# Two modulation blocks of a one-core layer stack moved from TensorE in the FFN to VectorE beside the output tiles

## The chip, the cores and the metric

One core of one Trainium2 chip runs one program. The metric is the device time of one launch in microseconds; less is better.

## The reference, cut to what matters

The input has 256 tokens of width 2048. A first block (pooling, convolution and gated branches, then an FFN of inner width 5504) is followed by two layers of a second block, which also carry a 256-token context beside the tokens. Everything is float32. The part that the change touches is the modulation of the second block:

```python
for l in range(DEPTH_2):
    shift, scale, gate = jnp.split(sc @ w_ada[l] + b_ada[l], 3, axis=-1)
    shift_c, scale_c, gate_c = jnp.split(scc @ w_ada[l] + b_ada[l], 3, axis=-1)
    h = rms(x, norm_w[l]) * (1.0 + scale[:, None]) + shift[:, None]
    hc = rms(xc, norm_w[l]) * (1.0 + scale_c) + shift_c
    ...
    x = x + gate[:, None] * merge_out(o_a, o_b, o_c, z, w_out[l])
    if not last:
        ...
        xc = xc + gate_c * merge_out(oa_c, ob_c, oc_c, z_c, w_out[l])
```

`sc` and `scc` are vectors of length 2048 (SiLU of `c` and `c_ctx`), so each product with `w_ada[l]` (2048 x 6144) is a matrix times a vector: 50 MB of weights a layer, read once, for two result vectors. Layer 1 is the last, so its context is not updated and its gate is needed for the tokens alone, while its shift is needed for tokens and context.

## The kernel before, in words

**The stream of weights.** All weights stand in one DRAM array in the order of use, cut into quarters of 128 x 1024 float32 (512 KB). SyncE loads quarter n into slot n mod 8 of `raw` as soon as quarter n-8 has been used (`weights_used`, L830; the few loads outside its loops are L844). For an ordinary quarter ScalarE writes the rounded high part `whi` (L865, four slots, three quarters ahead) and VectorE the remainder `wlo` (L1330, written over `raw`); TensorE then multiplies high by high, high by low and low by high. "hi" and "lo" below are these two conversions. A tile is 128 output channels and mostly takes two quarters.

**The modulation** has 24 blocks of 512 columns, of 8 quarters each. They are worked off in two ways:

- In the five FFN groups (`MOD_GROUPS`, `weave`, `mod_quarters` at L2215) a quarter needs no conversion: TensorE multiplies it by the columns `cs`, two quarters at a time, between two tiles. After 8 quarters VectorE copies the rows (L1745), TensorE transposes them (`mod_fold`, L2224), and VectorE sums them into `ada_t` (L1754, L1758). An FFN group has 16 up tiles, then 16 down tiles of one quarter each. A list says how many modulation quarters follow each tile; the last group has 32 of them, the other four 24 each: 128 quarters, that is 16 blocks.
- As rows on VectorE: a quarter holds half of the input for 128 output columns, and one `tensor_tensor_reduce` ("a product" below, with the reading of its accumulator) multiplies it by the broadcast vector and sums it, started from the bias or from the first half's sum. This is `gate0_products` beside the tiles of c0 (L1843), `gate1_products` beside those of c1 (L1857) and `row_products` beside layer 0's output tiles (L2112). A shift row of layer 1 needs two products a quarter (tokens and context), a gate row of layer 1 one.

TensorE holds back the last matmul of a tile that has such rows until the products are made (`gate0_mods`, `gate1_mods`, `gate_mods`), since that matmul also releases the rows' slots.

**Layer 0's output tiles** (out0: 16 tiles, each 48 matmuls of 512 columns) have `MOD_OUT` quarters of rows: none at tile 0, then 2, 2, 3 repeated to tile 13, 2 at tile 14, none at tile 15. `OUT_ROWS` alternates one shift row (two products a quarter) with one gate row (one product), 48 products in all. Per tile t, VectorE does in this order: the products of tile t, lo of quarters 2t+2 and 2t+3, the scaling of X by `fin_rst` (L2082), and then, once TensorE has finished tile t, `out_tile` (L2097) and a drain. GpSimd adds one square per tile (L2760).

**Layer 1's output tiles** (out1: 16 tiles, each 16 matmuls of 512 and 16 of 256 columns, `wide_chunk`, L2186 and L2187) have no rows. VectorE does lo of 2t+3 and 2t+4, then `out_tile` (L2091, L2093). The first 6 of 16 chunks of tiles 0 and 1 are computed inside the attention of heads c; `out_chunks` finishes them, and `tiles` does the rest, in a loop of four tiles a turn from tile 4 on. The stream's first 8 quarters of out1 are in their slots before out1 begins.

c1 has 16 quarters of gate rows 8 to 15, beside its 11 tiles (`C1_WEAVE`).

## Time and profile before

| | us |
|---|---|
| median of 3 runs (lowest, highest) | 3282.17 (3281.78, 3285.78) |
| the profiled execution's own time | 3282.73 |
| its span, first to last instruction | 3280.9 |
| PE busy | 3241.9 |
| VectorE busy | 2276.1 |
| ScalarE busy | 1431.5 |
| bytes read from HBM | 550.33 MB |

The profiled execution is 0.56 us above the median, and 1.8 us of its time lie outside the span. TensorE's granted clock is 0.999 of full over the whole span. PE stands for TensorE's matmuls, DVE for VectorE, ACT for ScalarE, POOL for GpSimd and SP for SyncE; a "q" behind a name is the engine's sequencer. Start times count from the first instruction of the span. An idle time in square brackets lies before the row's instruction and names what ended it.

### The profile page before, as it was taken

How to read it: one execution, taken by the hardware profiler on the slowest of the kernel's cores; microseconds unless marked ns; L12 is line 12 of the kernel's file. 1: busy time of each engine (PE TensorE's matmuls, PEld its weight loads, DVE VectorE, ACT ScalarE, POOL GpSimd, SP SyncE). 2: the span in 40 equal slices, each digit the busy share in tenths (PEclk: the TensorE clock that was granted, in tenths of full speed). 3: DMA queues.
4: the chain of work that ended last, by engine and by line, in shares of the span. 5: the costliest groups of instructions: out<-in, count | busy, mean ns of one | idle time of the engine just before them, and what ended most of it. 6: DMA issues, size and time to landing. Idle time of an engine off the chain costs nothing.

```text
span 3280.9 us, 56206 instructions
## 1 busy us (share of the span) xinstructions
PE 3241.9 (99%) x20346; PEld 2780.6 (85%) x20346; DVE 2276.1 (69%) x3372; ACT 1431.5 (44%) x2193; POOL 611.7 (19%) x552
## 2 busy tenths in 40 slices
PE   8999999999999999999999999999999999999999
PEld 8999999998987787898888787778878888888878
DVE  7887877567776677776765566667568776775865
ACT  5444445545443343453543433532352453453353
POOL 4999930111440000000300000000001100000000
PEclk9999999999999999999999999999999999999999
DMA  6555555565577777777733222134325543333435
GB/s 219 183 182 181 186 186 183 185 211 185 198 250 253 253 251 263 242 249 271 262 103 100 75 90 76 54 124 149 109 85 206 204 149 116 129 97 122 165 106 172
DMA packets 159872, 559.78 MB, mean 171 GB/s; under 512 B 17552, under 2 KB 23840, under 8 KB 159264
## 3 DMA queue, kind: packets, MB, share of 16 engines
q1 hardware_dynamic: 154144, 534.67, 48.4%
q0 software_dynamic: 5504, 22.04, 2.0%
q8 instruction: 151, 2.47, 0.3%
q14 instruction: 73, 0.60, 0.1%
HBM read 550.33 MB, written 6.31 MB: 170 GB/s over the span
## 4 chain that ended last, share of the span: by engine, by line
PE 91%; DVE 4%; ACT 2%; DVEq 1%; issue 1%; DMA 1%; ACTq 1%; POOL 0%; SPq 0%
PE psum L2159 17%; PE psum L2163 17%; PE psum L2160 17%; PE psum L2186 15%; PE psum L2187 7%; PE psum L2370 4%; PE psum L2521 2%; PE psum L2547 2%; PE psum L2532 2%; PE psum L2215 2%; PE psum L2371 2%; DVE wlo L1330 1%; PE psum L2290 1%; DVEq L1316 1%; PE psum L2478 1%
## 5 line engine op out<-in xcount | busy, mean ns | idle before, releaser
L865 ACT ACTIVATE whi<-raw 128x1024 fp32r<-128x1024 f32 (+3 forms) x844 | 864.6, 1030 | 982.5 <-PE psum L2163 538.8
L1330 DVE TENSOR_TENSOR wlo<-raw,whi 128x1024 fp32r<-128x1024 f32 (+3 forms) x844 | 1027.9, 1225 | 372.2 <-ACT whi L865 342.0
L2159 PE MATMUL psum<-hcat,whi 128*128 128x256 f32 (+1 forms) x3436 | 1125.8, 328 | 7.2 <-DVE wlo L1330 3.5
L2163 PE MATMUL psum<-hcat,wlo 128*128 128x256 f32 (+1 forms) x3436 | 1109.7, 323 | 2.0 <-DVE gate_half L1857 1.5
L2160 PE MATMUL psum<-hcat,whi 128*128 128x256 f32 (+1 forms) x3436 | 1109.3, 323 | 0.0
L2186 PE MATMUL psum<-hcat,whi 128*128 128x512 f32 x2048 | 725.8, 398 | 0.1
L2159 PEld LDWEIGHTS psum<-hcat,whi 128*128 128x128 f32 x3436 | 653.2, 190 | 78.1 <-issue 25.6
L2163 PEld LDWEIGHTS psum<-hcat,wlo 128*128 128x128 f32 x3436 | 653.0, 190 | 53.8 <-issue 2.3
L2160 PEld LDWEIGHTS psum<-hcat,whi 128*128 128x128 f32 x3436 | 653.6, 190 | 49.3 <-issue 0.7
L2187 PE MATMUL psum<-hcat,wlo 128*128 128x256 f32 x2048 | 573.5, 280 | 0.0
L2186 PEld LDWEIGHTS psum<-hcat,whi 128*128 128x128 f32 x2048 | 384.5, 188 | 107.3 <-issue 17.2
L2187 PEld LDWEIGHTS psum<-hcat,wlo 128*128 128x128 f32 x2048 | 386.6, 189 | 0.1
L2721 POOL TENSOR_SCALAR tap<-glu,par 128x255 f32<-128x255 f32 (+9 forms) x150 | 203.8, 1358 | 0.3 <-issue 0.3
L2370 PE MATMUL psum<-thirdcat,whi 128*128 128x512 f32 x512 | 182.9, 401 | 0.0
L2708 POOL TENSOR_TENSOR thirdcat<-tmp,thirdcat 128x256 fp32r<-128x256 f32 x43 | 51.3, 1193 | 617.8 <-ACT thirdcat L919 617.8
L2723 POOL TENSOR_TENSOR conv<-conv,tap 128x255 f32<-128x255 f32 (+9 forms) x150 | 149.2, 994 | 22.1 <-issue 0.3
L2371 PE MATMUL psum<-thirdcat,wlo 128*128 128x256 f32 x512 | 142.9, 279 | 0.0
L2370 PEld LDWEIGHTS psum<-thirdcat,whi 128*128 128x128 f32 x512 | 96.1, 188 | 39.7 <-DVE X L1712 9.2
L1361 DVE RECIPROCAL rst<-rst 128x512 f32<-128x512 f32 (+1 forms) x39 | 106.8, 2738 | 27.5 <-ACT rst L894 27.5
L2760 POOL TENSOR_TENSOR racc<-racc,rsq 128x256 f32<-128x256 f32 (+1 forms) x64 | 79.9, 1248 | 244.3 <-ACT rsq L931 221.8
L1893 DVE COPY qkv<-psum 128x512 f32<-128x512 f32 (+1 forms) x78 | 49.5, 635 | 107.6 <-PE psum L2163 107.5
L1951 DVE TENSOR_REDUCE stat<-psum 128x2 f32<-128x1024 f32 x78 | 81.6, 1046 | 34.6 <-PE psum L2521 30.5
(305 smaller groups left out, 3610.7 us busy)
## 6 DMA issues: line engine op xcount, KB each, us to landing
raw<-in_stream SPq DMA_DIRECT2D x978, 512.0 KB, 4.1
raw<-in_stream SPq DMA_DIRECT2D x18, 384.0 KB, 3.0
raw<-in_stream SPq DMA_DIRECT2D x24, 256.0 KB, 2.9
resid_dram<-X POOLq DMA_DIRECT2D x2, 2048.0 KB, 9.4
crow<-c_dram POOLq DMA_DIRECT2D x4, 1024.0 KB, 9.3
bias<-in_natten POOLq DMA_DIRECT2D x16, 256.0 KB, 2.9
X<-resid_dram POOLq DMA_DIRECT2D x4, 1024.0 KB, 6.2
raw<-in_stream SPq DMA_DIRECT2D x16, 192.0 KB, 2.6
```

Source lines behind the costliest of these rows:

```text
L865: act.activation(whi[:, c % HI_SLOTS, 0:n], raw[:, slot, 0:n], ACT.Copy).then_inc(hi_ready, 1)
L1330: vec.tensor_tensor(wlo[:, slot, 0:n], raw[:, slot, 0:n], whi[:, c % HI_SLOTS, 0:n].bitcast(F32), ALU.subtract).then_inc(lo_ready, 1)
L1361: vec.reciprocal(r, r)
L2159: pe.matmul(dst, h, cat[:, kk, c0:c0 + width], start=(q == 0 and k == 0), stop=False)
L2160: pe.matmul(dst, h, cat[:, kk, c0 + loff:c0 + loff + width], start=False, stop=False)
L2163: last = pe.matmul(dst, l_, cat[:, kk, c0:c0 + width], start=False, stop=(q == nq - 1 and k == nch - 1))
L2186: pe.matmul(psum[:, bank, :].rearrange("p (l c) -> p l c", l=2), h, both, start=first, stop=False)
L2187: return pe.matmul(psum[:, bank, 0:S], l_, both[:, 0, :], start=False, stop=last)
L2370: pe.matmul(psum[:, bank, :], h, thirdcat[:, kk, :], start=first, stop=False)
L2371: return pe.matmul(psum[:, bank, 0:S], l_, thirdcat[:, kk, 0:S], start=False, stop=last)
L2721: pool.tensor_scalar(tap[:, t % 2, 0:S - t], pick(glu, c, 0, S - t), wt, None, ALU.mult)
L2723: pool.tensor_tensor(pick(conv, c, t, S), pick(conv, c, t, S), tap[:, t % 2, 0:S - t], ALU.add)
```

## The change

Layer 1's gate rows leave out0; all 16 of its shift rows are made there instead (64 products in place of 48, in the same 32 quarters). c1 now makes gate rows 0 to 7 and out1 makes gate rows 8 to 15: 16 new quarters in out1's stream (two behind tile 1, two behind tile 2, one behind each of tiles 3 to 14), with one product each. Two blocks (16 quarters) leave the last FFN group, which keeps 16. The stream's length stays the same. In out1 TensorE's and ScalarE's loops become straight code, and the last chunk of each tile that has rows waits for them.

```diff
-MOD_FFN = [0, 2, 2, 0, 2, 2, 2, 0, 2, 2, 0, 2, 2, 2, 0, 2] + [0] * LATE + [2, 0] * 5 + [0] * 3
 MOD_FEW = [0, 2] * 8 + [0] * LATE + [0, 2, 0, 0, 2, 0, 0, 2, 0, 2, 0, 0, 0]
-MOD_GROUPS = [MOD_FEW if g < FF_GROUPS - 1 else MOD_FFN for g in range(FF_GROUPS)]
+MOD_LEAST = [0, 2, 0, 0, 2, 0, 0, 2, 0, 0, 2, 0, 0, 2, 0, 0] + [0] * LATE + [2, 0, 0, 2, 0, 0, 2] + [0] * 6
+MOD_GROUPS = [MOD_FEW if g < FF_GROUPS - 1 else MOD_LEAST for g in range(FF_GROUPS)]
...
-OUT_BLOCKS = [4 * D // 512 - 2, 4 * D // 512 - 1]
+OUT_BLOCKS = [*range(3 * D // 512, 4 * D // 512)]
...
-_shift, _gate = [4 * b + i for b in OUT_BLOCKS for i in range(4)], [5 * KD + t for t in range(KD // 2)]
-OUT_ROWS = [(j, 2 - n, half_) for some in zip(_shift, _gate) for n, j in enumerate(some) for half_ in range(2)]
-C1_ROWS = [5 * KD + t for t in range(KD // 2, KD)]
+OUT_ROWS = [(4 * b + i, half_) for b in OUT_BLOCKS for i in range(4) for half_ in range(2)]
+LAST_ROWS = [5 * KD + t for t in range(KD)]
 C1_WEAVE = weave([2] * 11, [1, 1, 2, 1, 2, 1, 2, 1, 2, 1, 2])
+OUT1_WEAVE = weave([2] * KD, [0, 2, 2] + [1] * (KD - 4) + [0])
...
                 if l:
-                    plain(f"out{l}", 32, 8, peel=1)
+                    plain("out1", 32, 32)
...
-                        s, (j, n, half_) = Q0["out0"] + pos, OUT_ROWS[a]
+                        s, (j, half_) = Q0["out0"] + pos, OUT_ROWS[a]
                         vec.wait_ge(raw_in[s % SLOTS], 16 * (s // SLOTS + 1))
-                        for c in range(n):
+                        for c in range(2):
...
-                def out_tiles(i):
-                    for k in range(8):
-                        lo(C0["out1"] + k + AHEAD, 8 * i)
-                        if k % 2 == 1:
-                            out_tile(1, 4 * i + k // 2, BANK[T0["out1"] + k // 2], Q0["out1"] + k, 8 * i)
-                            vec.drain().then_inc(x_tile, 1)
-
                 if l:
-                    out_tiles(0)
...
+                    for t, e in enumerate(OUT1_WEAVE):
+                        gate1_products("out1", e, KD, row_product.rearrange("p (b c) d -> p b c d", c=1)[:, t % 2])
+                        lo(C0["out1"] + 2 * t + AHEAD)
+                        lo(C0["out1"] + 2 * t + 1 + AHEAD)
+                        out_tile(1, t, BANK[T0["out1"] + t], Q0["out1"] + e["pos"] + 1, 0)
+                        vec.drain().then_inc(x_tile, 1)
...
                     if rows and kk == KD - 1:
-                        pe.wait_ge(gate_mods, rows[-1][1] + 1)
+                        pe.wait_ge(gate1_mods if l else gate_mods, (KD if l else 0) + rows[-1][1] + 1)
...
                         if kk % 8 == 7:
-                            last.then_inc(weights_used, 1)
+                            last.then_inc(weights_used, 1 + (len(rows) if kk == KD - 1 else 0))
...
                 if l:
-                    for t in range(2):
-                        out_chunks(l, t, Y_EARLY, KD)
-                    tiles("out1", 16, 4, hcat, 0, 2 * S, w, skip=2, k0=Y_PLACE, wide=True)
+                    for t, e in enumerate(OUT1_WEAVE):
+                        out_chunks(l, t, Y_EARLY if t < 2 else 0, KD, rows=e["mods"])
                     continue
```

The rest of the diff renames `gate1_products`'s arguments (it takes the phase's name, the first row and the scratch it writes to), sets the phases' lengths, and puts the quarters into the stream in the new order.

## Rows read from the trace of the kernel before

**Rows 1.** The page, part 1: busy us (share) xinstructions of each engine.

```profile
PE 3241.9 (99%) x20346; PEld 2780.6 (85%) x20346; DVE 2276.1 (69%) x3372; ACT 1431.5 (44%) x2193; POOL 611.7 (19%) x552
```

**Rows 2.** Three stretches: span, each engine's busy us (instructions), clock, DMA share, GB/s.

```profile
2458.00:2599.00 141.00, 141.00 (x625) 116.68 (x624) 115.14 (x155) 36.68 (x53) 23.80 (x14) 1.00 0.60 209
3199.50:3272.00 72.50, 72.50 (x412) 62.86 (x412) 43.31 (x53) 25.52 (x25) 0.00 (x0) 1.00 0.56 184
1472.00:1622.00 150.00, 150.00 (x1107) 128.34 (x1106) 106.28 (x175) 68.08 (x95) 34.01 (x23) 1.00 0.79 273
```

**Rows 3.** Waits of PE over the whole span: us in total, times, longest us.

```profile
PE psum L2163 <- DVE gate_half L1857: 1.5, 1, 1.5
...
PE psum L2634 <- DVE ada_t L2112: 1.0, 1, 1.0
```

**Rows 4.** The same view of the last FFN group, modulation matmuls of L2215 alone.

```profile
1472.00:1622.00 150.00, 17.04 (x128) 2.52 (x128) 1.00 0.79 273
```

**Rows 5.** Chain that ended last, last FFN group: start us, us, what.

```profile
1502.91 0.99 PE psum L2215 x8
1509.86 0.99 PE psum L2215 x8
1522.56 0.99 PE psum L2215 x8
1529.50 0.44 PE psum L2224 x4
```

**Rows 6.** PE in order of time at the end of that group: start us, us.

```profile
1621.78 0.60 PE L2224 MATMUL psum<-con,arow 128*128 128x128 f32 x4
1622.14 0.36 PE L2267 MATMUL psum<-hcat,whi 128*128 128x256 f32 x1
```

**Rows 7.** PE in order of time, 3.3 us later.

```profile
1625.48 0.67 PE L2290 MATMUL psum<-racc,con 128*128 128x256 f32 x2 [0.23 <-POOLq L2816]
```

**Rows 8.** VectorE in order of time, one output tile (the eighth) of layer 0.

```profile
2522.45 0.88 DVE L2097 SCALAR_TENSOR_TENSOR X<-psum,ada_t,X 128x256 f32<-128x256 f32 x2 [1.71 <-PE psum L2163]
2523.57 1.29 DVE L2112 CUSTOM_DVE_ANT_0 row_product<-raw,crow,par 128x1024 f32<-128x1024 f32 x1 [0.24 <-issue]
...
2524.99 2.10 DVE L2112 CUSTOM_DVE_ANT_0 row_product<-raw,crow_ctx,par 128x1024 f32<-128x1024 f32 x1
...
2529.85 0.08 DVE L2112 DVE_READ_ACCUMULATOR2_ANT ada_t<- 128x1 f32 x1
...
2532.12 0.48 DVE L2082 SCALAR_TENSOR_TENSOR X<-X,par,fin_rst 128x256 f32<-128x256 f32 x1
2533.34 0.88 DVE L2097 SCALAR_TENSOR_TENSOR X<-psum,ada_t,X 128x256 f32<-128x256 f32 x2 [0.73 <-PE psum L2163]
```

**Rows 9.** Waits of all engines during layer 0's output tiles (2445 to 2620 us).

```profile
DVE X L2097 <- PE psum L2163: 17.0, 11, 3.6
...
DVE wlo L1330 <- ACT whi L865: 1.3, 4, 0.4
```

**Rows 10.** VectorE in order of time during layer 1's output tiles.

```profile
3197.27 2.36 DVE L1330 TENSOR_TENSOR wlo<-raw,whi 128x1024 fp32r<-128x1024 f32 x2
...
3204.12 0.48 DVE L2091 SCALAR_TENSOR_TENSOR X<-psum,ada_t,X 128x256 f32<-128x256 f32 x1 [0.51 <-PE psum L2187]
...
3205.30 1.23 DVE L1330 TENSOR_TENSOR wlo<-raw,whi 128x1024 fp32r<-128x1024 f32 x1
...
3209.77 0.48 DVE L2091 SCALAR_TENSOR_TENSOR X<-psum,ada_t,X 128x256 f32<-128x256 f32 x1 [0.51 <-PE psum L2187]
```

**Rows 11.** ScalarE in order of time at the same place.

```profile
3194.93 2.01 ACT L865 ACTIVATE whi<-raw 128x1024 fp32r<-128x1024 f32 x2 [0.54 <-PE psum L2187]
...
3206.94 1.06 ACT L865 ACTIVATE whi<-raw 128x1024 fp32r<-128x1024 f32 x1 [1.76 <-PE psum L2187]
```

**Rows 12.** DMA issues of layer 1's output tiles: xcount, KB each, median us to landing.

```profile
raw<-in_stream SPq DMA_DIRECT2D x20, 512.0 KB, 4.3
```

**Rows 13.** The same of the last FFN group.

```profile
raw<-in_stream SPq DMA_DIRECT2D x77, 512.0 KB, 5.3
```

More of the change, by code:

```diff
@@ L157 @@
     PHASES += [(f"z{_l}", 2 * _n[0] + Z_MODS[_l], _n[0]), (f"a{_l}", 24, 12), (f"za{_l}", 2 * _n[1] + row_mods(f"za{_l}"), _n[1]),
-               (f"b{_l}", 20, 10), (f"zb{_l}", 2 * _n[2] + row_mods(f"zb{_l}"), _n[2]), (f"c{_l}", 22 + (2 * len(C1_ROWS) if _l else row_mods("c0")), 11), (f"kvb{_l}", 12, 12),
-               (f"qb{_l}", 9, 9), (f"out{_l}", 32 + (0 if _l else sum(MOD_OUT)), 16)]
+               (f"b{_l}", 20, 10), (f"zb{_l}", 2 * _n[2] + row_mods(f"zb{_l}"), _n[2]), (f"c{_l}", 22 + (KD if _l else row_mods("c0")), 11), (f"kvb{_l}", 12, 12),
+               (f"qb{_l}", 9, 9), (f"out{_l}", 32 + (KD if _l else sum(MOD_OUT)), 16)]
 Q0, T0 = {}, {}
@@ L202, in _converted @@
             own = {pos for e in Z_WEAVE[l] for pos, _ in e["pre"] + e["mods"]}
-        elif name in ROW_WEAVE or name in ("c1", "out0"):
-            own = {pos for e in ROW_WEAVE.get(name, C1_WEAVE if name == "c1" else OUT_WEAVE) for pos, _ in e["mods"]}
+        elif name in ROW_WEAVE or name in ("c1", "out0", "out1"):
+            own = {pos for e in dict(ROW_WEAVE, c1=C1_WEAVE, out0=OUT_WEAVE, out1=OUT1_WEAVE)[name] for pos, _ in e["mods"]}
         of += [Q0[name] + k for k in range(nq) if k not in own]
@@ L1845, in gate0_products, with gate1_products @@
                     last.then_inc(gate0_mods, 1)
-            def gate1_products(e):
+            def gate1_products(name, e, first, out):
                 for pos, a in e["mods"]:
-                    s, (t, half_) = Q0["c1"] + pos, divmod(a, 2)
-                    j = C1_ROWS[t]
+                    s, (t, half_) = Q0[name] + pos, divmod(first + a, 2)
+                    j = LAST_ROWS[t]
                     vec.wait_ge(crow1_in, 16)
@@ L2622, in out_chunks @@
                         pe.wait_ge(lo_ready, s + kk // 8 + 1)
-                    if kk in [first for first, _ in YCAT]:
+                    if t < 2 and kk in [first for first, _ in YCAT]:
                         pe.wait_ge(ycat_lo, len(YCAT) * l + sum(first <= kk for first, _ in YCAT))
                     if rows and kk == KD - 1:
-                        pe.wait_ge(gate_mods, rows[-1][1] + 1)
+                        pe.wait_ge(gate1_mods if l else gate_mods, (KD if l else 0) + rows[-1][1] + 1)
                     h, l_ = weight(s + kk // 8, P * (kk % 8))
@@ L2904, in _stream @@
     rows_c = rows[ROW_OF].transpose(2, 0, 1, 3).reshape(-1, P, QW)
-    rows_out = np.concatenate([rows[j, :, half_][None] for j, _, half_ in OUT_ROWS])
-    rows_c1 = rows[C1_ROWS].transpose(0, 2, 1, 3).reshape(-1, P, QW)
+    rows_out = np.concatenate([rows[j, :, half_][None] for j, half_ in OUT_ROWS])
+    rows_last = rows[LAST_ROWS].transpose(0, 2, 1, 3).reshape(-1, P, QW)
     def put_woven(weave_, tiles_, mods):
@@ L2950, in _stream @@
         if l:
-            put(oq)
+            put_woven(OUT1_WEAVE, oq, rows_last[KD:])
         else:
```

9 lines of the change are left out of this document (3 added, 6 removed).

## The prediction

> **What bounds the kernel now.** I read the page first. TensorE is busy for 3241.9 of 3280.9 us [rows 1], so what leaves TensorE shortens the kernel, as long as nothing else has to wait for the engine that takes it. VectorE takes it, so the second question is how much room VectorE has at the three places of the change. The view of three stretches [rows 2] says that TensorE is busy without a gap in layer 0's output tiles, in layer 1's and in the last FFN group, while VectorE is at 115.1 of 141 us, 43.3 of 72.5 and 106.3 of 150. An average doesn't tell whether another product fits, because VectorE works in order and waits for TensorE at the end of every tile. So I read on in the waits of the first stretch and in VectorE's order of time, tile by tile; their rows come with the terms below. TensorE already waits for products at two places, 1.5 us in c1 and 1.0 us at out0's tile 1 [rows 3].
>
> **What leaves the FFN.** The last group has 128 modulation matmul records, 8 for each pair of quarters, so 16 pairs [rows 4]; 8 pairs go. The price of one comes from the spacing of three pairs: 6.95 us across one tile and a pair, 12.70 us across two tiles and a pair [rows 5]. So a tile takes 5.75 and a pair 1.20 us, and eight take 9.6 us. Two of four folds go too, at 0.44 us where they stand in the chain [rows 5]. I credit only one: the last of the four stands behind the last tile [rows 6], and 3.3 us later TensorE waits 0.23 us for GpSimd's sum [rows 7], which comes from the tile before and not from the fold, so that wait grows by most of what the fold gives up. Sum: -10.0 us (-9.6 without any fold, -10.5 with both). TensorE never waits in this group [rows 2], so no wait is there to take the matmuls' place, and VectorE and the queue of SyncE's loads get less to do there (two copies and sums, 16 loads). The pair behind the last up tile goes too, which covered the last piece that GpSimd makes for the down tiles; the first seven chunks of three down tiles still cover it (21 chunks, each the 16th part of a tile's 5.75 us, 7.5 us in all), and if they didn't, it would cost no more than that pair's 1.2 us.
>
> **What out0 gets.** 16 more products, all at tiles 2 to 14 (tile 1 keeps its four). Between the starts of two products lie 1.42 us (2523.57 to 2524.99 [rows 8]), the reading of the accumulator among them; the second there is stretched to 2.10 us by GpSimd's sum of the tile, of which there is one a tile whatever the products. So 16 x 1.42 = 22.7 us of work are added to VectorE. Its slack from tile 2 to tile 14 is what it waited for TensorE, 17.0 us in 11 waits, and at most 1.3 us for ScalarE [rows 9]. So VectorE's work exceeds the room by 22.7 - 17.0 - 0.7 = 5.0 us, if no slack is wasted, taking half of the wait for ScalarE as usable.
>
> To see what TensorE feels of it I carried four rules through the tiles. TensorE's tile takes 10.89 us (2522.45 to 2533.34, the starts of two out_tiles [rows 8]). VectorE starts its products 1.12 us after the start of the last out_tile (2522.45 to 2523.57), has its first lo 1.14 us behind the last product, and comes to the next out_tile 2.83 us behind it (2.27 for two lo and 0.56 for the scaling). TensorE's tile t ends no sooner than 0.33 us after its products (one of 48 matmuls, 0.23, and 0.1 for the signal, my estimate), and tile t+1 starts no sooner than the lo of quarter 2t+2. For each tile I kept the duration measured there with its long instruction (thirteen tiles, of which [rows 8] show one) and added 1.42 us per new product. With the old counts the rules give tile 14's end at 2598.6 us, where the trace has 2598.62. With the new ones a tile with 2 quarters needs 10.2 to 10.5 us of VectorE, one with 3 needs 13.1 to 13.4, so three tiles need about 34 us against TensorE's 32.7. VectorE falls back by 1.1 to 1.4 us in every three tiles, and TensorE waits at two places in each: 0 to 0.8 us for the products before the last matmul of the 3-quarter tile, and 0.9 to 1.4 us for the first lo behind it. Tile 15 starts at 2603.8 instead of 2598.2: **+5.6 us**. With 1.36 or 1.50 us a product it is +5.0 or +6.6; with 0.2 us more or less a tile, +7.4 or +4.5.
>
> **What out1 gets.** Per tile TensorE takes 5.65 us (3204.12 to 3209.77 [rows 10]). VectorE's own work is 1.18 us from the start of an out_tile to the next lo (3204.12 to 3205.30), two lo of 1.14 each, and now one product of 1.42: 4.9 us, so it keeps up from tile 3 on, with 0.7 us to spare. Tiles 1 and 2 have two products. Tile 0 ends at 3194.9 (ScalarE is released by it [rows 11]), and tile 1, of which only 10 chunks are left, at 3198.4. But VectorE comes free from tile 0 at 3197.27 [rows 10], so two products end at 3200.2 and the last chunk at 3200.65: 2.3 us late. Tile 2 then has its products at 3206.95 (two lo, an out_tile and two products after 3200.2) where its matmuls would be ready for them at 3205.9: 1.1 us late; tile 3 is 0.2 us late, and the rest is on time. **+3.6 us.**
>
> This holds while the loads come in time. Three quarters a tile are 1.57 MB in 5.65 us, 278 GB/s, where now 184 are moved [rows 2]. A quarter takes a median of 4.3 us to land in out1 now [rows 12] and 5.3 us in the last FFN group [rows 13], which moves 273 GB/s. The first quarter of tile t+3 takes the slot of the second of tile t, so it is asked for at the end of tile t. It has then to land, to pass hi (1.06 [rows 11]) and lo (1.14), and behind it come the out_tile and the products for which tile t+2 waits, 10.86 us after the request. That leaves 10.86 - 1.06 - 1.14 - 1.18 - 1.52 - 0.1 = 5.9 us for landing. At 4.3 us I get +3.6, at 5.3 +5.2, at 5.9 +6.4. I take 4.3: the requests come two and one at a time, spread over the tile, as in out1 now, while the FFN group's come in larger bursts. The least is 2.3 us (tile 1 alone). The last tile has no rows, so the end behind it stays.
>
> On the landing the Trainium skill ("DMA: Bandwidth & Descriptors", Anatomy of one DMA) has its own figure: about 2.0 us fixed plus the bytes over 436 GB/s, so some 3.2 us for a quarter as an estimate. By it out1 would lose 3.1 us instead of 3.6 and the sum be 0.5 us lower. The rows here say 4.3, and I go by them.
>
> **Edits at nothing.** c1 keeps 16 quarters and 16 products, only of other rows. The straight code of out1 is hidden as out0's is, where TensorE runs straight code without a gap [rows 2]; a loop turn saved may give back 0.1 us. The gates that out1 makes are made in order ahead of the out_tile that reads them. Scratch for out1's products is in SBUF as at L2112.
>
> **Sum.** -10.0 + 5.6 + 3.6 = -0.8 us. On the profiled execution's 3282.73 us that is 3281.9; on the median, 0.56 us lower, **3281.4 us**. About 0.2%, or 6.6 us, is what a measurement of this kernel can tell from no change, so the forecast is "no difference": the FFN's gain is given back beside the output tiles. By the bounds (-10.5 to -9.6, +4.5 to +7.4, +2.3 to +6.4) this case reaches from 3278.5 to 3286.4.
>
> **Rivals.**
> - *VectorE has the room.* If the averages count (VectorE at 82% in out0, 60% in out1) and the order within a tile doesn't, nothing is given back: -10.0, 3272.2 us. For it: waits of VectorE for TensorE in 11 of 13 tiles [rows 9]. Against it: their sum is 17.0 us, less than the 22.7 added. Chance 0.13.
> - *Slower: the ring of slots in out1.* If quarters land 7 us after the request instead of 4.3, the loop over two tiles (request, landing, hi, lo, out_tile, product) is longer than two tiles. Each microsecond above 5.9 then costs half a microsecond a tile, over twelve tiles, and the late loads of the first tiles come on top: the same steps give +13.7 for out1, in all +9.3, 3291.5 us. It decides from 5.9 us on, and reaches a total above +6.6 at 6.6. For it: 5.3 us at 273 GB/s [rows 13]. Against it: the median there is still below the threshold, and DMA engines are at 79% of their time [rows 2]. Chance 0.10.
> - *The FFN doesn't give the time.* If the loads pace the last group (79% DMA share), the removed matmuls leave waits: at worst 0 instead of -10.0, so +9.2, 3291.4 us. Against it: no idle time of TensorE in the stretch, and the loads become 16 fewer. Chance 0.05.
> - The forecast's case has 0.72.
>
> **Numbers.** The range goes from 3275.5 to 3289.5: my case with its bounds, and the part of the rivals in which a stall is half missing or half as large again. Outside lie most of the first rival and the ends of the two others, about 0.2. Faster by over 0.2%: 0.14 (the first rival and a little of mine). Slower: 0.14 (the two others, less what stays within 6.6 us). Same: 0.72.
>
> **What would show it.** In the profile after: 64 matmul records of L2215 in the last FFN group, and out0's first tile about 10 us earlier. The products of out0 x64 with VectorE's waits for TensorE at L2097 down from 17.0 us to nearly nothing; TensorE idle at its tiles' last matmul and first matmul, 5 to 6 us in all, in pairs around tiles 3, 6, 9 and 12. In out1 two waits of TensorE of about 2.3 and 1.1 us at tiles 1 and 2 and none later, with quarters landing in 4 to 5 us. The forecast is wrong if out0's stretch grows by less than 3 or more than 8 us, if out1 shows waits at every second tile, or if the FFN group shrinks by less than 9 us.

## Result, and the profile after

The changed kernel takes 3286.73 us (median of 20 runs, 3283.54 to 3290.07) where the kernel before took 3281.98 beside it (20 runs, 3280.18 to 3285.78): +4.8 us, a ratio of 1.0015 [1.0009, 1.0020]. Run again on another chip it was +7.2 us, 1.0021 [1.0012, 1.0030]. The forecast was -0.8 us, no difference. The time lies inside the range and within 0.2%, but it grew, by more than its interval, where I had the gain and the loss cancel.

The profiled execution took 3283.54 us, the shortest of the 20, with a span of 3281.7 us. The page, part 1 (answers to [rows 1]), then the three stretches of [rows 2], moved to where they now lie (the first is the last FFN group, which I end at 1611 where it has ended; the second and third are layer 0's and layer 1's output tiles):

```profile
PE 3233.7 (99%) x20274; PEld 2778.3 (85%) x20274; DVE 2314.0 (71%) x3426; ACT 1430.1 (44%) x2193; POOL 612.1 (19%) x552
```

```profile
1472.00:1611.00 139.00, 139.00 (x1027) 125.14 (x1026) 104.84 (x167) 66.34 (x93) 33.63 (x23) 1.00 0.70 231
2449.00:2590.00 141.00, 138.05 (x602) 112.54 (x601) 129.89 (x179) 34.64 (x51) 23.09 (x14) 1.00 0.59 204
3199.50:3272.00 72.50, 69.82 (x403) 60.80 (x403) 60.16 (x80) 27.40 (x26) 0.00 (x0) 1.00 0.81 289
```

TensorE lost 8.2 us of busy time, and the span did not get shorter. In the FFN group it still never waits. In both output stages it now does: 141.00 busy of 141 has become 138.05, and 72.50 of 72.5 has become 69.82, while VectorE rose from 115.1 to 129.9 us and from 43.3 to 60.2. In out1 the DMA share went from 0.56 to 0.81.

The waits of PE over the whole span (answers to [rows 3]; us in total, times, longest), then VectorE's waits from the start of out0 on. The last row is before's, for the same load:

```profile
PE psum L2181 <- DVE ada_t L1857: 4.6, 2, 2.7
...
PE psum L2629 <- DVE ada_t L2112: 2.7, 1, 2.7
```

```profile
DVE X L2082 <- DMA X<-in_ctxT: 3.0, 1, 3.0
...
DVE X L2097 <- PE psum L2158: 1.7, 5, 0.7
```

```profile
DVE X L2082 <- DMA X<-in_ctxT: 1.4, 1, 1.4
```

VectorE's waits for TensorE at L2097 are down from 17.0 us [rows 9] to 1.7, as the working said: its slack is used up. But TensorE's wait at out0's tile 1 grew from 1.0 to 2.7 us, which no step of mine had. The cause stands in the other row: VectorE waits 3.0 us, where it was 1.4, for context rows that are loaded into X ahead of tile 0. The issues before and after:

```profile
X<-in_ctxT POOLq DMA_DIRECT2D x2, 1024.0 KB, 9.7
```

```profile
X<-in_ctxT POOLq DMA_DIRECT2D x2, 1024.0 KB, 11.3
```

The first is before's row, the second after's. The same load is issued at the same distance from its neighbours and lands 1.6 us later. In all eleven traces with the shortened FFN it took 11.0 to 11.8 us (median of the two loads), in all five with more quarters there (before's three, b4 and c3) 9.3 to 9.7. Why is open.

**Where the time went, by stage.** Five landmarks of VectorE, the same in each kernel, cut the span: its reciprocal behind the FFN, the update of X at out0's first tile and at its fifteenth, and at out1's first and last. Lengths in us, one profiled execution each:

| kernel | start to reciprocal | to out0 | out0 | to out1 | out1 |
|---|---|---|---|---|---|
| before | 1627.1 | 821.7 | 149.8 | 597.1 | 81.9 |
| before, again (b1) | 1627.3 | 821.6 | 149.8 | 599.1 | 80.3 |
| after | 1616.1 | 823.4 | 155.4 | 598.2 | 85.4 |
| after, again (a1) | 1616.3 | 822.9 | 156.4 | 598.2 | 86.6 |

Against the mean of the two traces of before (1627.2, 821.7, 149.8, 598.1, 81.1) the mean of the two of after has -11.0, +1.5, +6.1, +0.1 and +4.9: together +1.6 us. The two profiled executions of the changed kernel were the shortest of their 20 and 11, those of before were not, so this is the lower end of the difference.

The traces of the experiments below have most stages unchanged, and they show how far one stage scatters. Means over all traces in which a stage is as in the kernel of its row (number of traces in brackets; the changed kernel's out0 with all 64 products, its out1 with all 16, none filled):

| kernel | start to reciprocal | to out0 | out0 | to out1 | out1 |
|---|---|---|---|---|---|
| before | 1627.0 (3) | 821.6 (3) | 149.8 (2) | 598.4 (3) | 80.8 (3) |
| changed | 1617.2 (11) | 823.2 (11) | 155.8 (6) | 598.7 (11) | 86.8 (4) |
| difference | -9.8 | +1.6 | +6.0 | +0.3 | +6.0 |

Together +4.1 us, near the first pair of medians (+4.8) and inside the interval of each (+3.0 to +6.6 and +3.9 to +9.8). The two pairs above came out lower by chance: their first stage, 1616.1 and 1616.3 us, is at the short end of eleven (1616.1 to 1619.1, the same work in each), and before's out1 of 81.9 us is the long one of three. In that trace TensorE takes 5.65 us a tile there and in b1 5.55, both at a granted clock of 1.00; why is open.

**What fills the rest.** The granted clock is below 1.00 in short stretches, 1 us windows in the trace of after behind the wait at out0's tile 1 (columns: window, its length, PE busy (instructions), clock, DMA share, GB/s):

```profile
2444.00:2446.00 2.00, 0.00 (x0) 1.00 0.78 301
2446.00:2447.00 1.00, 0.86 (x2) 0.56 0.06 25
2447.00:2448.00 1.00, 1.00 (x3) 0.50 0.02 8
2448.00:2449.00 1.00, 1.00 (x4) 0.50 0.20 29
2449.00:2450.00 1.00, 1.00 (x5) 0.73 0.86 287
2450.00:2451.00 1.00, 1.00 (x6) 1.00 0.99 381
```

TensorE did nothing for 2.7 us, and then the granted clock was 0.50, the 1.2 GHz level, before it came back to 1.00 (2.4 GHz). The shortfalls of the four windows add up to 0.44 + 0.50 + 0.50 + 0.27 = 1.7 us of full clock. Such stretches, nearly all with 1.7 us lost (a3 has one of 3.4), start in or just behind TensorE's gaps of 1.8 to 3.3 us, at most places in some executions and not in others: before at 844 (gap 2.2 us), before again at 2672 (2.9) and 3065 (1.9) and not at 844, after at 2446 and 2668. At out0's tile 1 it stands in all nine traces whose gap there is 2.2 us or more, and in none of the others (gap 0.7 to 1.0 us, or filled, or gone). Over the timed executions the mean clock is 0.9992 for before (33 runs, beside a1) and 0.9980 for after (20), and the changed kernel's time goes with it: 3284.1 us on average at 0.999, 3287.1 at 0.998, 3289.4 at 0.997. So the change had added a place where the clock falls, and two more gaps in out1 of that size, and the question for the experiments was how much of the loss is that, and how much is VectorE, its order, and the loads.

### The profile page after: what moved, and what is told of

It is laid out like the page before. It is cut to its first block, busy times and chain, and to the rows that moved or that the text cites. A ratio compares the mean times of both kernels' runs of the same rounds, so it can differ in the third digit from the quotient of the medians.

```text
span 3281.7 us, 56108 instructions
## 1 busy us (share of the span) xinstructions
PE 3233.7 (99%) x20274; PEld 2778.3 (85%) x20274; DVE 2314.0 (71%) x3426; ACT 1430.1 (44%) x2193; POOL 612.1 (19%) x552
## 4 chain that ended last, share of the span: by engine, by line
PE 89%; DVE 5%; ACT 2%; DVEq 1%; issue 1%; DMA 1%; ACTq 0%; POOL 0%; SPq 0%
PE psum L2154 17%; PE psum L2158 17%; PE psum L2155 17%; PE psum L2181 14%; PE psum L2182 7%; PE psum L2365 4%; PE psum L2516 2%; PE psum L2542 2%; PE psum L2527 2%; PE psum L2366 2%; PE psum L2210 2%; DVE wlo L1330 1%; DVE row_product L2112 1%; DVEq L1316 1%; PE psum L2285 1%
```

## Experiments

A name such as a1 or c1 is that of a run here; the kernel's own c1 is called "the stage c1". Twelve runs of variants and two more on what was still open. "Against before" is always the difference of medians to the kernel before on the same chip in the same job; the changed kernel stands at +4.8 and +7.2 by this measure, about +6.

**1. The changed kernel again (a1).** No edit.

> The changed kernel again, for a second trace and more executions. Theory A (half clock behind gaps): my terms were right in the profiled execution (FFN -9 to -10, out0 +5.7, out1 +3.5), and the median is 3 us above it because TensorE falls to its 1.2 GHz level for about 3.6 us, at a price of about 1.8 us, behind some of the waits of over 1.9 us; there are three more of these than before (out0 tile 1: 2.7 us, out1 tile 1: 2.7, tile 2: 1.9). Then the median is again 3286 to 3287, and executions with a lower mean clock are the longer ones. Theory B (VectorE's order costs more in most executions): this trace shows out0 growing by 8 us or more with the clock at 2.4 GHz. Theory C (the FFN gives less than 9 us): the last FFN group shrinks by less than 8 us.

Measured 3288.29 us (11 runs), +7.2, 1.0021 [1.0012, 1.0030]. The effect is there again, and the spread of one kernel (3285.5 to 3290.7) is a little larger than before's (3279.8 to 3284.8). The expectation has the two waits of out1 the wrong way round: tile 1's is 1.9 us, tile 2's 2.7.

**2. out0's products back to 48 (a2).**

```diff
+ m = 8 if c and a // 2 % 2 else QW
- vec.tensor_tensor_reduce(row_product[:, (a + c) % 2, :], raw[:, s % SLOTS, :], row[...QW], ...)
+ vec.tensor_tensor_reduce(row_product[:, (a + c) % 2, 0:m], raw[:, s % SLOTS, 0:m], row[...m], ...)
```

> The changed kernel with 48 full products in out0 as before (the context product of every second row reads 8 columns instead of 1024, so half of layer 1's context shift is left out). A: out0's 5.7 us come back and hardly any dip, since the wait at tile 1 stays: 3281.0, -5.7 against the changed kernel. B: -9 or more, 3277.5. C: -5.7 too.

Measured 3282.36, +1.3 against before, 5.9 below a1. out0's stage is 150.9 us, where it was 149.8 before and 156.4 in a1: VectorE's 16 added products cost 5.5 us there. The load of X stays late (3.1 us of wait, TensorE's gap at tile 1 2.8 us), and 1.1 us of out0 stays. It lies between the updates of tiles 1 and 2, where the clock is at 0.50; from there to tile 14 the stage takes 130.6 us, as in before.

**3. out1's products made tiny, its loads kept (a3).**

```diff
+ m = 8 if name == "out1" else QW
- vec.tensor_tensor_reduce(out..., raw[:, s % SLOTS, :], crow1[...QW], ...)
+ vec.tensor_tensor_reduce(out...[:, 0:m], raw[:, s % SLOTS, 0:m], crow1[...m], ...)
```

> The changed kernel with out1's 16 products on 8 columns instead of 1024 (layer 1's gate rows 8 to 15 are left out in the main), the loads as they are. A: the 3.5 us of waits and the half clock behind the two gaps go: -3.5 and another -1 to -3, 3279.5 to 3282. B and C: -3.5 alone, 3283.2. If the loads set out1's pace and not the products, less than -2.

Measured 3286.18, +5.1 against before, only 2.1 below a1, and out1 still takes 86.6 us. VectorE in order of time shows why:

```profile
3197.96 0.23 DVE L1858 CUSTOM_DVE_ANT_0 row_product<-raw,crow,par 128x8 f32<-128x8 f32 x1 [0.31 <-issue]
...
3198.48 1.22 DVE L1330 TENSOR_TENSOR wlo<-raw,whi 128x1024 fp32r<-128x1024 f32 x1
3204.53 1.23 DVE L1330 TENSOR_TENSOR wlo<-raw,whi 128x1024 fp32r<-128x1024 f32 x1 [4.84 <-ACT whi L865]
```

The product takes 0.23 us, and the next lo still comes 4.84 us late, because ScalarE has waited 6.6 us for the quarter's load. TensorE waits 3.2 us at this place, and behind that the clock stands at 0.50 for longer than elsewhere: 3.4 us of full clock lost, where neither trace of the changed kernel has any in out1. So the equal length of the stage doesn't say that the products cost nothing. By the median they cost 2.1 us, the smaller part of out1's loss.

**4. out1's quarters spread more evenly (a4):** none at tile 1, two at tiles 7, 11 and 14.

```diff
-OUT1_WEAVE = weave([2] * KD, [0, 2, 2] + [1] * (KD - 4) + [0])
+OUT1_WEAVE = weave([2] * KD, [0, 0, 1, 1, 1, 1, 1, 2, 1, 1, 1, 2, 1, 1, 2, 0])
```

> The changed kernel with out1's 16 rows behind tiles 2 to 14, two each only at tiles 7, 11 and 14, so that tile 1 (of which 10 chunks are left) has none. The same work and loads. A: the waits at tiles 1 and 2 (2.7 and 1.9 us) go, VectorE stays in time except for up to 1 us behind the double tiles: -3 for the waits and -1 to -2.5 for the clock, 3280.5 to 3283. B and C: -3, 3283.7.

Measured 3287.15, +6.1 against before, 1.1 below a1; out1 85.8 us. TensorE's 4.4 us of waits for products have become 4.0 in three places, at tiles 7, 11 and 14, the three with two quarters of rows. Moving the pairs only moved the waits.

**5. The kernel before again (b1).** No edit.

> The kernel before, looked at once more, unchanged. In its first profile the granted clock falls to its lower level (0.50) once, from 844 to 849 us, behind a TensorE gap of 2.2 us. Theory A (a gap of about 2 to 3 us is followed, in some executions, by 3 to 4 us at half clock, some 1.7 us lost each): its gaps are 10.0, 3.0, 2.2 us and smaller ones, so this execution shows 0 to 2 such stretches, at those gaps and nowhere else, and none at out0's tile 1 (gap 1.0 us). Theory B (nothing but the order of VectorE's work makes the change slower): any stretch at half clock is equally frequent in both kernels and may stand anywhere.

3283.1 us; its row stands in the table above, its stretches at half clock in the text under it. There is none at out0's tile 1, where the gap is 0.9 us. It has one at 3065, in the stage c1, behind a gap of 1.9 us at a wait that the change doesn't touch. A third stands at the very end (3280), where TensorE has finished; the expectation had none there.

**6. One product more at out0's tile 1, in the kernel before (b2).** It is computed twice; nothing else changes.

```diff
-for c in range(n):
+for c in (0, 0, 1) if a == 1 else range(n):
```

> The kernel before, with one of out0's first products (tile 1) computed twice, so that TensorE's gap there of 1.0 us becomes 1.0 + 1.42 = 2.4 us; VectorE has 17.0 us of slack behind it and takes the lag up, so nothing else moves. Theory B: the time grows by 1.4 us. Theory A: the gap is now of the size behind which the clock falls, so in the profile the granted clock is 0.50 for 3 to 4 us behind tile 1 (2445 to 2452) if this execution is one of those, and the median grows by 1.4 plus up to 1.7 us: 2 to 3.1 us. A second bound: if the larger gap changes the clock's mean over the whole program, by more than 4 us.

Measured 3285.41, +3.2 against before (ratio 1.0007 [0.9998, 1.0016]). TensorE's gap is 2.2 us in place of 1.0, and behind it the clock falls. PE in order of time, then windows over the same place:

```profile
2456.09 0.50 PE L2634 MATMUL psum<-hcat,whi 128*128 128x512 f32 x1 [2.24 <-DVE ada_t L2112]
```

```profile
2456.00:2457.00 1.00, 0.91 (x3) 1.00 0.15 57
2457.00:2458.00 1.00, 0.73 (x3) 0.56 0.00 0
2458.00:2459.00 1.00, 1.00 (x4) 0.50 0.73 213
2459.00:2460.00 1.00, 1.00 (x3) 0.50 0.95 377
2460.00:2461.00 1.00, 1.00 (x5) 0.74 1.08 397
2461.00:2462.00 1.00, 1.00 (x6) 1.00 0.85 225
```

In b1 the windows of the same matmuls have 1.00 throughout:

```profile
2457.00:2458.00 1.00, 1.00 (x5) 1.00 0.51 111
2458.00:2459.00 1.00, 1.00 (x6) 1.00 0.86 336
2459.00:2460.00 1.00, 1.00 (x6) 1.00 0.99 373
```

The stage out0 went from 149.8 to 152.6 us, so +2.8: 1.2 of gap and 1.6 of clock. The median's +3.2 agrees, though its interval alone would not exclude 1.4. This is the cleanest price of the clock: one more VectorE instruction of 1.42 us in front of a wait cost twice its length, in the one trace of it.

**7. No gap at out0's tile 1, in the changed kernel (b3):** its four products on 8 columns.

```diff
+ m = 8 if a < 2 else QW
```

> The changed kernel, with the four products of out0's tile 1 on 8 of 1024 columns, so that they cost VectorE about 0.2 instead of 1.42 us each and TensorE's gap of 2.7 us there goes. VectorE comes 4 to 5 us earlier into tile 2, and as its lag builds up over 13 tiles, that lead is kept in part. Against the changed kernel's 3288.3 on the same chip: theory A says 2.7 (gap) + up to 1.7 (half clock behind it) + 1 to 2 (lead): -4.0 to -6.4. Theory B says 2.7 + 1 to 2: -2.7 to -4.7, with the granted clock behind tile 1 the same as in the changed kernel. My forecast's steps had tile 1's wait at 1.0 us and the first lag only from tile 3: by them -1.0 to -3.

Measured 3283.53, +1.3 against before, 3.5 to 5.9 below the changed kernel. out0 takes 151.9 us and has no stretch at half clock. This holds the gap, the clock and VectorE's lead together and does not part them. Its out1, unchanged, has a gap of 3.1 us with half clock behind it and takes 88.7 us, the longest of the four traces with that schedule.

**8. A middle version (b4).** All five FFN groups with 24 quarters (120 in all, between the changed kernel's 112 and before's 128); out0 with 12 shift rows and 4 gate rows (56 products); out1 with 8 quarters, at tiles 4 to 11.

```diff
-MOD_GROUPS = [MOD_FEW if g < FF_GROUPS - 1 else MOD_LEAST for g in range(FF_GROUPS)]
+MOD_GROUPS = [MOD_FEW] * FF_GROUPS
-OUT_BLOCKS = [*range(3 * D // 512, 4 * D // 512)]
+OUT_BLOCKS = [*range(3 * D // 512 + 1, 4 * D // 512)]
-OUT1_WEAVE = weave([2] * KD, [0, 2, 2] + [1] * (KD - 4) + [0])
+OUT1_WEAVE = weave([2] * KD, [0] * 4 + [1] * 8 + [0] * 4)
```

> A version between the two: all FFN groups with 120 quarters (8 of the 16 pairs' quarters back to the last group against the changed kernel, 4 pairs fewer than before); out0 makes 12 shift rows (48 products) and 4 of the last output rows (8 products), 56 in place of 64; out1 has only 8 quarters, one at each of the tiles 4 to 11, so neither tile 1 nor tile 2 waits for products and the loads start 4 tiles later. By the sizes measured so far: FFN -5.0 against before, out0 about +1.0 to +2.5 (a2, at 48 products: +1.1), out1 0 to +1, late ctxT and gap at tile 1 as in the changed kernel +1.7 to +3. Theory B: -1 to -3 against before, 3278.5 to 3280.5. Theory A: one place of half clock fewer than in the changed kernel, but out0's tile-1 gap keeps one, so about 1 us more than that: 3279.5 to 3281.5. If out1's loss is from its loads whatever the products, it shows as waits of ScalarE on DMA at tiles 4 and later, and TensorE's out1 stretch is over 83 us instead of 81.9.

Measured 3281.62, -0.6 against before (0.9996 [0.9987, 1.0005]). FFN -3.0 where I expected -5.0, out0 +3.3, out1 81.1 us with no wait of TensorE for a product. Both differences went the wrong way. The FFN's lies within the scatter: c3 below has the same FFN groups and is 5.8 us shorter than before there. The time is not parted from before's.

**9. The three waits filled (c1).** The changed kernel with its whole work, and matmuls that do nothing but keep TensorE busy until the products come: 10 at out0's tile 1, 14 and 18 at out1's tiles 1 and 2.

```diff
+FILL = {(0, 1): 10, (1, 1): 14, (1, 2): 18}
...
 if rows and kk == KD - 1:
+    if (l, t) in FILL:
+        pe.wait_ge(psum_free, FREE[ts + 1])
+        for _ in range(FILL[l, t]):
+            pe.matmul(psum[:, BANK[ts + 1], 0:w], whi[...], hcat[:, kk, 0:w], start=True, stop=True)
     pe.wait_ge(gate1_mods if l else gate_mods, ...)
```

> The changed kernel with its whole work, and with matmuls added that only fill TensorE's three waits for products: 10 of 512 columns (2.3 us) at out0's tile 1 (gap 2.7), 14 of 256 columns (1.6 us) at out1's tile 1 (gap 1.9) and 18 (2.1 us) at its tile 2 (gap 2.7), into the bank of the next tile, which starts over. Nothing is taken away. Theory A (the granted clock falls to 0.50 for 3 to 4 us behind a gap of about 2 to 3 us): the gaps left there are 0.3 to 0.6 us, so no stretch at half clock stands behind these three places, the mean clock rises from 0.998 to 0.999, and the time falls by up to 1.7 us a place: 1.5 to 4 us less than the changed kernel's 3286.7 to 3288.3. Theory B (only the order of VectorE's work and the loads count): the same time within 0.7 us, or up to 0.5 more.

Measured 3286.68 (11 runs, 3286.06 to 3288.49), +4.3 against before. At out0's tile 1 (window, length, PE busy, clock; compare the rows of after above):

```profile
2444.00:2446.00 2.00, 2.00 (x10) 1.00 1.03 387
2446.00:2448.00 2.00, 1.18 (x5) 1.00 0.28 111
2448.00:2450.00 2.00, 1.74 (x8) 1.00 0.22 41
```

The clock stays at 1.00 behind all three places; the mean clock of the 11 executions is 0.9990, before's own. Adding 42 matmuls made the kernel no slower, and its spread went from 5.3 and 6.5 us to 2.4. But the time fell only from about +6 to +4.3, the low end of what I had expected, and by the intervals (1.0012 [1.0003, 1.0021] here) the two are not parted. By stage: out0 154.8 us, where six traces with all 64 products and the gap have 155.4 to 156.4, so 1.1 us less on average; out1 86.7, nothing less. So in out0, where VectorE soon has the next word, the lower clock costs about 1 of its 1.7 us. For out1 this trace gives no price: both traces of the changed kernel have 1.00 there as well. a2 and b3, with one such stretch in out1, have 86.6 and 88.7 us, the three without 85.4, 86.6 and 86.7. The clock explains a part of the changed kernel's scatter, and a smaller part of why it is slower.

**10. out1 without its 16 quarters (c2).** Neither loads nor products; FFN and out0 as changed.

```diff
-OUT1_WEAVE = weave([2] * KD, [0, 2, 2] + [1] * (KD - 4) + [0])
+OUT1_WEAVE = weave([2] * KD, [0] * KD)
```

> The changed kernel with out1's 16 quarters left out altogether, loads and products (the eight rows get a constant gate instead). FFN and out0 stay as changed. a3, which kept the loads and made the products small, came out 2.1 us below the changed kernel. Theory D (in out1 the loads cost most): out1 goes back to before's 80.3 to 81.9 us from 86.6, so -4.5 to -6 against the changed kernel, of which only 2 from the products. Theory B (the products alone): no more than a3's -2.1, -1.5 to -3. My forecast had +3.6 for out1: -3.6.

Measured 3279.80, -2.5 against before, 7 to 10 below the changed kernel. out1 is back at 80.3 us, the same stretch without a gap and with before's traffic:

```profile
3199.50:3272.00 72.50, 72.50 (x420) 63.93 (x419) 44.08 (x53) 25.61 (x25) 0.00 (x0) 1.00 0.59 184
```

So out1 costs 5 to 6 us, not 3.6, and with a3 (2.1 us less with the products tiny) the larger part hangs on the loads. The medians differ by 1 to 4 us more than the stage; the stages in front of it are unchanged, and that rest is not explained.

**11. The middle version, gate rows first (c3).** Tile 1 of out0 gets two products in place of four. The edit is against b4:

```diff
-    _some.insert(4 * _i + 3, (5 * KD + 8 + _i, 1))
+    _some.insert(4 * _i, (5 * KD + 8 + _i, 1))
```

> The middle version (b4, 3281.6 against 3282.2) with one more edit: in out0 each gate row (one product a quarter) goes ahead of its three shift rows, so tile 1 has 2 products in place of 4. VectorE is then 2.8 us earlier at tile 1, where TensorE waits 0.7 us in b4, and a little of the lag at later tiles may go as well: -0.7 to -2 against b4, so 3279.6 to 3281. If a gap of 0.7 us costs only itself (theory A: it is too short for the clock to fall), -0.7 at this place and the same number of stretches at half clock as in b4 (two in its profile).

Measured 3280.36, -2.0 against before by the medians, though the interval of the ratio (0.9996 [0.9987, 1.0005]) does not part it from before. Of the versions that do the whole work it stands best against before; out0 takes 152.1 us and TensorE has no wait for products there at tile 1.

**12. Both stages' products made small (c4),** the edits of a2 and a3 together.

> The changed kernel with 16 of out0's 64 products and all 16 of out1's on 8 of 1024 columns, all loads kept: VectorE's added work is gone. The rival of my prediction by which VectorE has the room would have the full 10 us: with VectorE's cost taken away the kernel should reach 3272. Theory B: a2 and a3 add up, -5.9 - 2.1 = -8.0 against the changed kernel, 3279 to 3280.5, the rest being what out1's loads, the late load ahead of out0 (1.4 us) and the clock take. If they add up to more than -10, the two stages' losses were not independent.

Measured 3280.98, -1.4 against before, 6 to 9 below the changed kernel: the two add up. With VectorE's added work gone the kernel does not reach 3272. TensorE's waits say what is left, both behind loads (a quarter at out1's tile 2, X's context rows at out0's tile 1):

```profile
PE psum L2183 <- DVE ada_t L1858: 3.0, 1, 3.0
...
PE psum L2631 <- DVE ada_t L2114: 2.3, 1, 2.3
```

**13. out1's quarters at tiles 4 to 14 (d1).** Whole work.

```diff
-OUT1_WEAVE = weave([2] * KD, [0, 2, 2] + [1] * (KD - 4) + [0])
+OUT1_WEAVE = weave([2] * KD, [0] * 4 + [2, 1, 2, 1, 2, 1, 2, 1, 2, 1, 1, 0])
```

> The changed kernel with its whole work; in out1 the 16 quarters stand at tiles 4 to 14 (two and one in turn) in place of tiles 1 to 14, so no load of theirs is asked for while X's residual comes in (two loads of 1 MB on GpSimd's queue) and the ring of slots starts full. c2 showed that the quarters of out1 cost 6 us with their loads, a3 that the products alone cost 2. Theory D1 (the quarters' loads are late because they meet the residual's at the start of out1, where ScalarE waits 6.0 us for one and TensorE 1.9 and 2.7 us for the products behind it): no wait of TensorE for products above 1 us, out1 81 to 83 us in place of 85.4 to 86.6, and -3 to -5 us against the changed kernel, 3283 to 3284. Theory D2 (three quarters a tile are too many for the ring at any tile, as in my prediction's slower rival): tiles with two quarters wait here too, by 0.5 to 1 us each, and out1 stays at 85 us or more.

Measured 3295.96 (5 runs), +14.4 against before, 1.0049 [1.0036, 1.0063]. My favourite (D1, the residual's loads in the way) fell clearly. The waits of PE, then VectorE in order of time:

```profile
PE psum L2181 <- DVE ada_t L1857: 6.2, 3, 2.8
PE psum L2181 <- DVE gate_half L1857: 5.1, 2, 2.6
```

```profile
3222.10 1.23 DVE L1330 TENSOR_TENSOR wlo<-raw,whi 128x1024 fp32r<-128x1024 f32 x1 [3.37 <-ACT whi L865]
...
3232.06 1.22 DVE L1330 TENSOR_TENSOR wlo<-raw,whi 128x1024 fp32r<-128x1024 f32 x1
3236.29 1.23 DVE L1330 TENSOR_TENSOR wlo<-raw,whi 128x1024 fp32r<-128x1024 f32 x1 [3.02 <-ACT whi L865]
```

Every two tiles, that is at every tile with two quarters of rows, a lo is 3 to 4 us late, and TensorE waits 1.2 to 2.8 us. The stage takes 95.8 us. In it the DMA engines are busy 71% of the time and a quarter lands in a median of 4.7 us. But the requests come in bursts: none from 3222.4 to 3228.1 us, then four within 2.8 us (3228.1, 3228.7, 3229.3 and 3230.9), and ScalarE's longest waits end with the third of such a burst, which lands after 5.3 to 6.2 us (the last wait with a second, after 6.8). A quarter can be asked for only when its slot has been used, and a tile that holds four quarters gives its slots back together, behind TensorE's wait. That is the mechanism of my slower rival, the ring of slots. I had let it decide by the landing time, from 5.9 us on. The stage's median is below that, and the loads that are waited for are around it.

**14. d1 with out0's tile 1 filled (d2).**

```diff
+FILL = {(0, 1): 10}
```

> d1 with ten filling matmuls of 512 columns at out0's tile 1 as in c1, whole work. c1 gave out0 154.8 us against 155.4 to 156.4 and left out1 as it was, where loads and VectorE set the pace and a lower clock cost nothing. Expected by that: out0 about 1.1 us shorter than in d1, out1 the same as in d1, so -0.5 to -1.5 against d1. If the clock behind that gap cost its full 1.7 us: -1.7.

Measured 3292.39 (6 runs), +10.9 against before, 3.6 below d1, more than either theory gives. By stage out0 is 0.7 us shorter (155.0 for 155.6) and out1 2.3 (93.6 for 95.8), which the filling does not touch. The profiled execution of d2 is its slowest of six. With five and six runs and a stage that scatters, I call this one inconclusive beyond out0's 0.7.

## Why the prediction was wrong

The kernel got slower where I had the gain and the loss cancel. Two things failed. Out1's +3.6 was too small: it stands on the step "I take 4.3" us for the landing of a quarter, and the load that tile 2's wait hangs on took 6.3; the stage costs +4.9 us (pairs) to +6.0 (all traces). And the sum has nothing for the context rows loaded into X, which land 1.6 us later, nor for the clock at 0.50 behind the longer gap at out0's tile 1. The FFN's term and out0's total came true, out0's partly by luck.

**The FFN: right.** 64 records of L2210 (L2215 before) stand in the last group:

```profile
L2210 PE MATMUL psum<-raw,cs x64: 592/605/617, 1474.9 to 1592.8; 128*32 128x512 f32 x64
```

The group's modulation is half of before's, TensorE never waits, and the stage ends 9.8 us sooner over all traces (11.0 in the two pairs) where I had -10.0. The rival "the FFN doesn't give the time" is out.

**out0: VectorE's mechanism right, the total partly by luck.** Forecast +5.6, measured +5.6 in the first pair and +6.1 over both. The updates of X at tiles 2 and 14, first in before, then in after:

```profile
2467.99 0.88 DVE L2097 SCALAR_TENSOR_TENSOR X<-psum,ada_t,X 128x256 f32<-128x256 f32 x2 [2.43 <-PE psum L2163]
...
2598.62 0.88 DVE L2097 SCALAR_TENSOR_TENSOR X<-psum,ada_t,X 128x256 f32<-128x256 f32 x2 [3.57 <-PE psum L2163]
```

```profile
2459.64 0.88 DVE L2097 SCALAR_TENSOR_TENSOR X<-psum,ada_t,X 128x256 f32<-128x256 f32 x2 [0.66 <-PE psum L2158]
...
2594.87 0.88 DVE L2097 SCALAR_TENSOR_TENSOR X<-psum,ada_t,X 128x256 f32<-128x256 f32 x2 [0.26 <-PE psum L2158]
```

These twelve tiles grew from 130.6 to 135.2 us, by 4.6, and a2 without the 16 products is back at 130.6. VectorE needs 10.2 us for a tile with two quarters (2472.70 to 2482.90) and 13.1 for one with three (2459.64 to 2472.70), and three tiles take 33.7 to 34.0 us where I had about 34. So this part is VectorE's, 1.0 us less than my recurrence had. The other 1.1 us lies between tiles 1 and 2 (10.8 us for 9.7), where the clock is at 0.50. From tile 0's update to tile 1's both kernels take 9.4 us: TensorE's longer gap there is the late load again, and it is counted ahead of out0. TensorE's waits show less than the growth, one of 0.7 us for the first lo behind each three-quarter tile and hardly any in front of a tile's last matmul:

```profile
PE psum L2154 <- DVE wlo L1330: 2.7, 4, 0.7
PE psum L2158 <- DVE ada_t L2112: 0.2, 1, 0.2
```

**In front of out0: a term missing.** +1.5 us, the late load of X. I had no step for it. The change does not touch it, and why it is late stays open; but before's trace had VectorE waiting 1.4 us for it at this place, so that any delay of it would be felt in full.

**out1: the wait I named, the wrong landing.** Forecast +3.6, measured +4.9 over two pairs, and 5 to 6 by c2. VectorE, ScalarE and TensorE at tiles 1 and 2:

```profile
3193.02 0.48 DVE L2091 SCALAR_TENSOR_TENSOR X<-psum,ada_t,X 128x256 f32<-128x256 f32 x1
...
3197.01 1.22 DVE L1330 TENSOR_TENSOR wlo<-raw,whi 128x1024 fp32r<-128x1024 f32 x1
3200.38 1.23 DVE L1330 TENSOR_TENSOR wlo<-raw,whi 128x1024 fp32r<-128x1024 f32 x1 [2.16 <-ACT whi L865]
3201.53 0.48 DVE L2091 SCALAR_TENSOR_TENSOR X<-psum,ada_t,X 128x256 f32<-128x256 f32 x1
```

```profile
3199.29 1.06 ACT L865 ACTIVATE whi<-raw 128x1024 fp32r<-128x1024 f32 x1 [6.02 <-DMA raw<-in_stream]
```

```profile
3197.15 0.50 PE L2181 MATMUL psum<-hcat,whi 128*128 128x512 f32 x1 [1.91 <-DVE ada_t L1857]
...
3205.65 0.50 PE L2181 MATMUL psum<-hcat,whi 128*128 128x512 f32 x1 [2.68 <-DVE ada_t L1857]
```

Tile 1 waits 1.9 us (forecast 2.3). Tile 2 waits 2.7 and not 1.1: VectorE stood idle for 2.16 us for hi, and hi for 6.0 us for its load. The loads of the first tiles land later than the stage's median, beside X's residual. The first two rows are after's issues from 3183 to 3205 us; the third is after's of 3192.2 to 3193.2, the last two that are asked for before ScalarE's wait; the last is before's of 3195 to 3199, at the same place:

```profile
raw<-in_stream SPq DMA_DIRECT2D x7, 512.0 KB, 5.2
X<-resid_dram POOLq DMA_DIRECT2D x2, 1024.0 KB, 5.7
...
raw<-in_stream SPq DMA_DIRECT2D x2, 512.0 KB, 6.0
```

```profile
raw<-in_stream SPq DMA_DIRECT2D x3, 512.0 KB, 6.3
```

The step that failed is "I take 4.3". It is the median of the whole stage, and from tile 3 on it came true (4.3 again, and no wait of TensorE there). The wait that came out 1.6 us longer than forecast, tile 2's, stands behind a load of 6.3 us (6.2 in a1). Tile 1's, which hangs on VectorE and no load, came out shorter. My own line said "at 5.3 +5.2, at 5.9 +6.4", and +4.9 to +6.0 is what came. The number to take stood in before's own trace: there the same first loads, without any new quarter, took 6.3 us in the median, and TensorE had enough tiles in store not to feel it. So I had the right sum and read the landing from the wrong stretch. The slower rival, the ring of slots, was judged rightly for one quarter of rows a tile. Where two stand at one tile, a4 and d1 show a wait at every such tile.

What makes the first loads late is not shown by a run. In all sixteen traces, before's and those without new quarters at the start of out1 among them, the two quarters asked for 1.5 and 2.2 us behind the second load of X's residual took 5.5 to 7.0 us, and quarters later in the stage a median of 4.1 to 4.7. So the new quarters don't make them late; the residual's load is beside them every time, and no run moved it.

On the landing the Trainium skill ("DMA: Bandwidth & Descriptors", Anatomy of one DMA) had given 3.2 us as an estimate. The page fits that figure to loads issued from GpSimd's queue, and the quarters go out on SyncE's. Single quarters came near it (3.1 us for the first of out1), but no stretch of out1 had a median below 3.9 us; the measurement decides.

**The clock: a mechanism missing.** A step of 0.001 in the mean clock goes with 2.3 to 3.0 us of the changed kernel's time. b2 shows the price of one stretch, 1.6 us beside a gap of 1.2, and c1 that with the three gaps filled the clock is before's and the slowest executions are gone. In out0 it costs about 1 us. What it costs in out1 is open. The stages' means over all traces account for +4.1 us of the medians' +4.8 and +7.2; whether the 3 us that are left on the second chip are more than noise, and whether they are the clock's, no run here shows. The sign was there to see: before's own trace has a stretch at 0.50 behind its gap of 2.2 us at 844, and I forecast a new wait of 2.3 us and priced it at 2.3 us.

**Rivals.** "VectorE has the room" fell by a2: with 16 products out the stage gave 5.5 us back. c4 adds that even without VectorE's work the other things leave nothing near 3272. The change did what it says, and the 10 us of the FFN are there; they are spent beside the output tiles.

## What to carry to other kernels

When work is moved beside a stage, take the landing time of its loads from the very tiles where the wait will stand (here the loads at the start of out1 took 6 us beside the residual's and 4.3 later), not from the stage's median; and where a ring of slots feeds the loads, look at how many requests come at once before counting bytes. Look also for waits on loads just ahead of the stage: they are felt in full when the load slips. A new wait of TensorE of 2 us or more has to be priced with what the granted clock does behind it, which the kernel's own trace shows, but only where TensorE and not VectorE or a load sets the next microseconds. And compare a median with a profiled execution only with its place among the timed ones in view: here the traces of the variants, taken together, gave the sum that the two pairs missed.

## What the runs showed of the hardware

- The granted clock goes to 0.50 (1.2 GHz) for 3 to 4 us behind a TensorE gap of 1.8 to 3.3 us, at 1.7 us of full clock each (once, in a3, 7 us and 3.4). At the same place it does so in some executions and not in others: behind the gap of 2.2 us at 844 in ten of sixteen traces. In after it fell as TensorE started again (2446.14), in b2 some 1 us later (2456.09, and the first window below 1.00 is 2457 to 2458). Gaps of up to 1.5 us were never followed by it, and neither was the one of 10 us at the start. Cost in time: 1.6 us where TensorE set the pace (b2), about 1 in out0 of the changed kernel (c1); in out1 no pair of traces prices it.
- Filling matmuls in front of a wait keep the clock at 1.00 and didn't lengthen the kernel where the wait is longer than they are: 42 of them, mean clock 0.9980 to 0.9990, spread 2.4 us for 5.3 and 6.5.
- A load of 512 KB that lands in 4.3 us in the middle of the stage took 5.5 to 7.0 us when asked for 1.5 to 2.2 us behind a load of 1 MB on GpSimd's queue, in all sixteen traces. And a stage can starve for loads with its DMA engines at 71%: the third request of a burst landed after 5.3 to 6.2 us, where the median was 4.7 (d1).
- The same code takes 1616.1 to 1619.1 us to the end of the FFN in eleven traces, and a tile of out1 5.65 us in one trace and 5.55 in another at the same granted clock. One pair of traces can't price a change of 5 us in 3280.
